# Gathering the last token tile of the first expert block from its normed fp32 rows

## The reference, cut to what matters

```python
h = layer_norm(ALPHA * x + mix, ln1_g, ln1_b)
logits = (h @ router_w + router_b)
top_v, top_e = lax.top_k(logits, 4)              # 4 of 32 experts
gates = softmax(top_v)
# each expert: its tokens in blocks; gu = xb @ w_gu[e] + b_gu[e]; clamped SwiGLU; act @ w_down[e] + b_down[e]
y = sum over the 4 experts of gate * expert(h)
x = layer_norm(ALPHA * h + y, ln2_g, ln2_b)
```

## Time and profile before

| what | value |
|---|---|
| median of the runs | 1566.97 us (1563.92 to 1567.91) |
| the profiled execution's own time | 1565.8 us |
| its span | 1564.1 us |
| PE busy | 1486.2 us (95%) |
| DVE busy | 476.1 us (30%) |
| ACT busy | 278.8 us (18%) |
| DMA moved | 507.65 MB, mean 325 GB/s |
| mean granted TensorE clock | 0.988 of full speed |

### The profile page before, as it was taken

The page is one execution under the profiler, slowest core; times in us unless marked ns, Lnnn a source line. Parts: engine busy times, 40 slices in busy tenths (PEclk is TensorE's granted clock), DMA queues, the critical chain, the costliest instruction groups (busy, mean ns, idle before and its releaser), DMA issues.

```text
span 1564.1 us, 20898 instructions
## 1 busy us (share of the span) xinstructions
PE 1486.2 (95%) x8226; PEld 757.5 (48%) x8227; DVE 476.1 (30%) x920; ACT 278.8 (18%) x618; POOL 110.6 (7%) x98
## 2 busy tenths in 40 slices
PE   9999998999998999899999999999899899899896
PEld 7777776655676775333333333333333333333332
DVE  3552455577450026421222122121121121121123
ACT  1222434532120003201010110100100100100102
POOL 1001222010050602000000000000000000000000
PEclk9999999999999999999999999999999999999998
DMA  6245487536238954999999999999999999999995
GB/s 206 108 162 170 142 264 232 182 123 219 81 119 253 301 215 170 376 428 427 428 427 428 428 428 429 429 429 428 428 429 428 429 428 428 428 428 429 429 429 237
DMA packets 105350, 507.65 MB, mean 325 GB/s; under 512 B 7575, under 2 KB 44031, under 8 KB 80575
## 3 DMA queue, kind: packets, MB, share of 16 engines
q1 hardware_dynamic: 100938, 499.37, 79.7%
q10 hardware_dynamic: 4360, 7.55, 1.5%
HBM read 491.18 MB, written 15.72 MB: 324 GB/s over the span
## 4 chain that ended last, share of the span: by engine, by line
PE 59%; DMA 26%; DVE 4%; ACT 1%; issue 1%; DVEq 0%; SPq 0%; ACTq 0%
DMA wGU<-in_w_gu 25%; PE ps L2289 15%; PE ps L1804 11%; PE ps L2294 10%; PE ps L1817 4%; PE ps L2107 3%; PE ps L2121 2%; PE ps L2134 2%; PE ps L2247 1%; PE ps L2228 1%; DMA ringS<-in_ssd_proj 1%; DVE up L1705 1%; DVE up L1707 1%; DVE act_values L1708 1%; PE ps L1880 1%
## 5 line engine op out<-in xcount | busy, mean ns | idle before, releaser
L2289 PE MATMUL ps<-wGU,xe 128*64 128x512 f32 x2048 | 454.7, 594 | 33.7 <-DMA wGU<-in_w_gu 33.0
L2289 PEld LDWEIGHTS ps<-wGU,xe 128*64 128x64 f32 x2048 | 143.8, 137 | 325.9 <-issue 257.3
L2294 PE MATMUL ps<-wD,aT 128*64 128x512 f32 x1024 | 226.8, 595 | 6.3 <-ACT aT L1266 6.3
L1804 PE MATMUL ps<-xT,ring 128*128 128x288 f32 x704 | 183.9, 417 | 6.2 <-ACT qT L1007 4.1
L1804 PEld LDWEIGHTS ps<-xT,ring 128*128 128x128 f32 x704 | 133.4, 194 | 47.6 <-issue 5.2
L2294 PEld LDWEIGHTS ps<-wD,aT 128*64 128x64 f32 x1024 | 70.7, 137 | 140.3 <-issue 127.9
L1705 DVE TENSOR_SCALAR up<-ps 128x512 f32<-128x512 f32 x32 | 22.1, 692 | 378.4 <-PE ps L2269 378.4
L1260 ACT ACTIVATE sg<-ps 128x512 f32<-128x512 f32 x32 | 19.1, 597 | 536.7 <-PE ps L2269 536.7
L1711 DVE COPY ysb<-ps 64x512 f32<-64x512 f32 x32 | 22.2, 694 | 282.4 <-PE ps L2298 282.4
L391 PE MATMUL ps<-xT,ring 128*128 128x288 f32 x320 | 78.1, 407 | 0.0
L2107 PE MATMUL ps<-ynT,ringS 128*128 128x288 f32 x256 | 65.2, 419 | 4.2 <-issue 4.0
(11 more groups left out here) (473 smaller groups left out, 1370.7 us busy)
## 6 DMA issues: line engine op xcount, KB each, us to landing
wGU<-in_w_gu SPq DMA_DIRECT2D x128, 2048.0 KB, 37.2
wD<-in_w_down SPq DMA_DIRECT2D x64, 2048.0 KB, 37.1
ring<-in_w_in SPq DMA_DIRECT2D x21, 2048.0 KB, 8.8
out<-hst SPq DMA_DIRECT2D x8, 1024.0 KB, 5.9
ringS<-in_ssd_proj SPq DMA_DIRECT2D x4, 2048.0 KB, 13.0
wbuf<-prompt_A_rows ACTq DMA_DIRECT2D x16, 384.0 KB, 4.0
out<-Sb SPq DMA_DIRECT2D x2, 2048.0 KB
ring<-in_hg_proj SPq DMA_DIRECT2D x2, 2048.0 KB, 8.5
```

Source lines behind the costliest of these rows:

```text
L1804: last = m.matmul(ps[:, b, 0:T], ring[c % 2][:, k, n * P:(n + 1) * P], xT[:, k, :], start=(k == 0), stop=(k == KD - 1))
L2289: last = m.matmul(ps[half[h], bank, :], xe[:, f, hx, :], wgu[n][:, k, col + CW * h:col + CW * h + CW], start=(i == 0 and k == 0), stop=False)
L2294: last = m.matmul(ps[half[h], B_Y, :], aT[:, k, i - 4, :], wdn[n][:, k, CW * h:CW * h + CW], start=(i == 4 and k == 0), stop=False)
```

## The change

- VectorE makes `psf`, an fp32 copy of tile 1's slice of the first selection matrix, just ahead of `psel`.
- TensorE no longer computes tile 1's remainder ahead of the first block. In the opening it gathers tile 1 by one fp32 product for each half of the columns, `psf x xres`, in the place of the six bf16 products; the table's product (L2305 before) comes behind it.
- The remainder of tile 1 (`residual`) is computed in `run(0)`, its first half ahead of weight piece 1 and its second half ahead of piece 2. ScalarE's two casts of it stand now behind the exponential of the gates and VectorE's two subtractions behind the gates `gm`. TensorE waits for them (`t_z`) ahead of the gather of block 1, between pieces 3 and 4.

```diff
@@ scalar
-                for n in range(2):
-                    act.wait_ge(t_q, 1 + n)
-                    a.copy(hp0[1][:, 1, CW * n:CW * n + CW], ps[:, 4 + n, :]).then_inc(t_c, 1)
-
                 act.wait_ge(m_x, 1)
                 a.copy(xs[:], ps[:, B_X, :]).then_inc(m_xs, 1)
                 act.wait_ge(m_xt, 1)
                 a.copy(xe[:].rearrange("p f h j -> p (f h j)"), ps[:, B_XT, :]).then_inc(m_xc, 1)
                 act.wait_ge(t_e, 1)
                 a.activation(gt4[:], gt4[:], ACT.Exp).then_inc(t_ex, 1)
+                for n in range(2):
+                    act.wait_ge(t_q, 1 + n)
+                    a.copy(hp0[1][:, 1, CW * n:CW * n + CW], ps[:, 4 + n, :]).then_inc(t_c, 1)
                 a.activation(yacc[:, 1, :], xres[:, 1, :], ACT.Copy, scale=ALPHA).then_inc(t_y, 1)
@@ vector
                 dstep(v.tensor_reduce(dsel[:], dsl[:], AX_X, ALU.add))
+                dstep(v.tensor_scalar(psf[:], jcol1[:], dsel[:, 1:2], None, ALU.is_equal))
                 v.tensor_tensor(psel[:], ...).then_inc(m_p, 1)
...
-                for n in range(2):
-                    cols = slice(CW * n, CW * n + CW)
-                    dve.wait_ge(t_c, 13 + n)
-                    v.tensor_tensor(hp0[1][:, 2, cols], ps[:, 4 + n, :], hp0[1][:, 1, cols], ALU.subtract).then_inc(t_z, 1)
...
+                (the same loop, behind the gates gm)
@@ tensor
-                for n in range(2):
+                def residual(n):
                     cols = slice(CW * n, CW * n + CW)
-                    pe.wait_ge(t_h, 4 + n)
                     m.matmul(ps[:, 4 + n, :], ident[:], xres[:, 1, cols], start=True, stop=False)
                     pe.wait_ge(t_c, 11 + n)
                     m.matmul(ps[:, 4 + n, :], nidb[:], hp0[1][:, 0, cols], start=False, stop=True).then_inc(t_q, 1)
@@ run(b, turn0, first, pair, opening=False)
+                        if opening and i in (1, 2):
+                            residual(i - 1)
...
+                            if opening:
+                                pe.wait_ge(t_z, 2)
@@ the opening on TensorE
                 pe.wait_ge(m_p, 1)
                 gather(2)
                 gather(0)
+                pe.wait_ge(t_h, 5)
+                for h in range(2):
+                    last = m.matmul(ps[half[h], B_X, :], psf[:], xres[:, 1, CW * h:CW * h + CW], start=False, stop=True)
+                last.then_inc(m_x, 1)
                 pe.wait_ge(t_eb, 1)
                 m.matmul(ps[0:1, 3, 0:64], ebc[0:64, 0:1], ident[0:64, 0:64], ...).then_inc(t_tb, 1)
-                pe.wait_ge(t_z, 2)
-                gather(1)
                 pe.wait_ge(m_xs, 1)
                 turn_x()
                 pe.wait_ge(m_ok, 1)
-                run(0, 0, 0, None)
+                run(0, 0, 0, None, opening=True)
```

More of the change, by code:

```diff
@@ L689, in build @@
         dsl = at("dsl", 196.5, [P, 3, E_])
+        psf = at("psf", 196.5, [P, BLK])
         gsel = at("gsel", 163, [P, 3, 2, BLK])
@@ L1722, in _ @@
                     dstep(v.tensor_reduce(gm[0:rows, t, :], eg[0:rows, t, :, :].rearrange("p k e -> p e k"), AX_X, ALU.add))
+                for n in range(2):
+                    cols = slice(CW * n, CW * n + CW)
+                    dve.wait_ge(t_c, 13 + n)
+                    v.tensor_tensor(hp0[1][:, 2, cols], ps[:, 4 + n, :], hp0[1][:, 1, cols], ALU.subtract).then_inc(t_z, 1)
                 dve.wait_ge(t_y, 3)
@@ L2254, in scatter, with run @@
                         (prompt(j, B_S + j % 3) if j < 4 else samples(B_S + j % 3)).then_inc(m_s, 1)
-                def run(b, turn0, first, pair):
+                def run(b, turn0, first, pair, opening=False):
                     pe.wait_ge(m_xc, b + 1)
```

## The result

The changed kernel takes 1568.37 us (median of 20 runs, 1566.41 to 1573.97), the kernel before 1565.06 (20 runs, 1562.80 to 1567.91). The ratio is 1.0023, interval 1.0015 to 1.0030: some 3.6 us slower (2.3 to 4.7), where 1.0 was forecast. By the 0.3% of the prediction that is no change, but the kernel is slower by more than the forecast had it, and the profile says where.

What follows compares the result with a forecast made beforehand. The expert stage's weight DMA stream was taken to bound the kernel, started by PE's first weight piece. A start 0.71 us later plus 0.3 for the remainder gave 1.0 us on 1566.97, hence 1568.0; range 1563.5 to 1571.0.

Steps and rivals of the forecast that it cites:

- the 0.3% of the prediction: Whole kernel's time: a change can be told from none at about 0.3%, 4.7 us.
- The start bounds the end, one for one: Weight stream: the end follows PE's start on the first weight piece one for one, up to 2.7 us forward.
- psf's cost: Opening, VectorE ahead of `psel`: one more instruction makes `psel` ready 0.27 us later, bounds 0.2 to 0.4.
- the pickup of the gather: Opening: PE, free of the remainder, begins to gather 0.06 us after `psel`, 0.69 us earlier than before.
- the table's product: Opening, behind tile 1's gather: its later place costs nothing, with 0.4 us to spare; bound 0 to 0.3.
- The clock under the gather: Opening: granted clock 0.50 for the whole gather, 3.71 us, so the first weight piece starts 0.71 us later.
- Rival (a): Gather in the opening: clock at full speed or back early in it; 0.8 us faster, 1566.2; chance 0.2.
- The remainder inside block 0: Ahead of weight pieces 1 and 2: products of 2.2 to 2.6 us delay the DMA issues, costing 0.3 us.
- Rival (b): First weight piece and the transposes ahead: the low clock reaches into them; +5.2 us, 1572.2; chance 0.08.
- ScalarE's and VectorE's covers: Block 0: their moved work stays hidden with 1.7 us; block 1's `psel` ready at start + 14.5, wanted at + 16.2.

Runs made afterwards that it cites:

- e12: Kernel before with ten idle bf16 products, all ahead of weight piece 0, so that the start itself is late; one run, 1566.0 us.
- e5: Changed kernel with 11 idle bf16 products behind the logits and the remainder's products back in the opening; ratio to before 0.9987, timed again 0.9992.
- e2: Changed kernel with idle bf16 products in the two pauses ahead of the gather (11 behind the logits, 16 behind the counts); ratio to before 1.0016.
- e4: Kernel before with ten idle bf16 products in block 0, five ahead of weight piece 1 and five ahead of piece 2; ratio to before 1.0015.
- e7: Kernel before with five idle bf16 products ahead of weight piece 1 alone; one run, 1569.1 us.
- e1: Changed kernel without TensorE's four remainder products in block 0, those output parts left out; ratio to before 1.0011.
- e8: Changed kernel with the remainder ahead of weight pieces 2 and 3 in place of 1 and 2; one run, 1567.5 us.
- e6: Kernel before with five idle bf16 products ahead of weight piece 2 alone; one run, 1564.6 us.

## Why the prediction was right or wrong

*The number.* The forecast of 1568.0 lies 0.4 us from the measured 1568.37, and that is luck. It was built on 1566.97, the median of three runs of before; twenty runs have 1565.06, 1.9 us lower. The change was put at 1.0 us and measured at 3.3 by the medians and 3.6 by the ratio. The two errors nearly cancel.

*The start bounds the end, one for one.* Right: e12's late start and e5's early one keep a stream of 902 us.

*psf's cost, the pickup of the gather, the table's product.* Right: `psel` 0.29 us later (4.52 behind L1613 for 4.23; 0.27 forecast), gather 0.67 us earlier against L1613 (0.69), the table's product hidden, with less to spare than 0.4 us.

*The clock under the gather.* Right for this pair of profiles: 0.50 to the end of the gather, 3.63 us for it (633.13 to 636.76; 3.71 forecast), 1.00 again under the transposes, start 0.65 later (0.71). e2 is the test: with work in the pauses the same gather takes 1.91 us and the start moves by 1.72. Rival (a) would have needed that. The Trainium skill's sentence (TensorE: Matmul & The Clock Gate, Part 1), that activity releases the throttle, agrees with these two granted clocks. That the sum came out to 0.06 us is luck again. It compares one execution with one, and the opening of before starts at other times in other executions: 9.71, 9.72, 9.75 (e12, up to its idle products), 10.26 (e4) and 10.72 (e7), 10.03 on average, by where the clock comes back. The changed opening has 10.36, 10.15 (e1) and 10.17 (e8), 10.23 on average. A later start by 0.2 us is what these eight show, not 0.65.

*The remainder inside block 0.* This is the term that failed: 0.3 us forecast, 2.2 measured. The step was "With a queue still delivering I lean to the low end and take 0.3 us", in a working that looked at the fifth issue alone, as the tightest. The fifth issue has two remainders against it, but the second and third follow a queue that has just been filled: in before they come 3.35 and 4.8 us ahead of the end of the previous piece, in after 1.8 and 2.6. These two pieces then lose 0.82 and 0.75 us, the fifth itself 0.19. The mechanism, issues that come too late for the queue, was the right one. The place and the size were wrong: the prediction counted a loss only where the queue runs dry, but the second and third lose although they are issued 1.8 and 2.6 us before that. In before the stretches behind the first issue (642.56) show how long a pickup lasts; the prediction's 2.5 us to a full flow is measured as nearly 3:

```profile
644.00:644.50 0.50, 0.50 (x6) 0.23 (x4) 0.45 (x3) 0.00 (x0) 0.00 (x0) 1.00 0.39 66
645.50:646.00 0.50, 0.50 (x4) 0.17 (x2) 0.25 (x2) 0.00 (x0) 0.00 (x0) 1.00 1.15 492
```

That a lead shorter than this pickup is what costs fits most of the pieces above but is not shown. The remainder was also priced as product time only, 1.1 to 1.3 us, and measured 1.36. e1 takes the term away, e4 brings it into the kernel before, e8 moves it.

*Rival (b)*, the low clock in the first weight piece, is not in the profile of after, but it is in one execution of e7. The Trainium skill's rule named with it (the monitor does not start afresh with a kernel) was a fair warning. Whether it makes up the 0.8 us between the profiles' 2.8 and the ratio's 3.6 is not shown; 2.8 lies within the ratio's interval.

*ScalarE's and VectorE's covers* held: the `psel` of block 1 is ready 14.8 us behind the start (14.5 forecast), TensorE wants it at 17.1 (16.2), and the fifth issue comes 24.7 us behind the start, 2.8 later than in before, of which the two remainders are 2.7. In e8, with the second remainder one piece later, the cover is gone.

In sum: start 0.65 for 0.71 (0.2 over several executions), stream 2.2 for 0.3.

## What to carry to other kernels

Work moved out of a pause and behind a prefetched stream is not free because the engine has a lead there: look at every issue that it delays, and at how long ahead of the previous transfer's end each one comes; here 2 MB pieces wanted about 3 us. And when a matmul is taken out of a pause on the way to a critical group, ask what clock that group will find: eleven idle bf16 products ahead of it brought the start to 8.7 to 8.9 us behind L1613, where before has 9.7 to 10.7; the edit alone did not. And read a shift of under 1 us from several executions, not from one pair.

## What the runs showed of the hardware that was not expected

- A stream of 2 MB pieces loses 0.1 to 1.1 us on a piece that is issued 1.6 to 2.6 us ahead of the end of the piece before (twelve cases), though the queue is never empty by the issues' times; GB/s falls from 428 to about 345 to 400.
- Two delays of about 1.3 to 1.4 us lose 2.2 us (after) or 3.2 (e4) by the span's end, one alone 0.0 (e6, piece 2) or 1.2 (e7, piece 1): the loss is not proportional to the delay.
- The end follows the slowest of the sixteen DMA engines. In e4 the volume is 2.2 us late and the end 3.2.
- The granted clock can fall just at the start of a dense stretch. In e7 it is 0.60 in the first half microsecond and 0.50 behind it, and 16 weight instructions take 5.35 us instead of 3.65:

```profile
639.00:639.50 0.50, 0.46 (x2) 0.31 (x4) 0.00 (x0) 0.50 (x1) 0.33 (x1) 0.60 0.24 98
640.00:642.00 2.00, 2.00 (x8) 0.76 (x6) 1.33 (x6) 1.97 (x4) 0.00 (x0) 0.50 0.02 8
```

```profile
639.04 5.35 PE L2296 MATMUL ps<-wGU,xe 128*64 128x512 f32 x16 [0.72 <-issue]
```

- The same opening code starts 9.71, 9.72, 10.26 and 10.72 us behind L1613 in before, e6, e4 and e7, by where the clock comes back; and L1613 itself lies between 625.5 and 630.7 us in the profiles. Differences under 1 us are seen in a profile against a mark, and hardly in the total.
